# Two probability maps, combined on ScalarE and GpSimd instead of VectorE

## What is computed

```python
s = einsum('bqhmd,bkhmd->bhmqk', qi, k) * ATTN_SCALE        # m: the two maps
s = where(k_pos[None, :] <= q_pos[:, None], s, NEG)         # causal
p = softmax(s, axis=-1)
attn = p[..., 0, :, :] - lam * p[..., 1, :, :]
o = einsum('bhqk,bkhe->bqhe', attn, v)
```

## Time and profile before

| | |
|---|---|
| median of 3 runs | 4023.01 us (4020.77 to 4033.34) |
| profiled execution | 4022.81 us, span 4021.0 us |
| mean granted TensorE clock | 0.911 |
| busy in the span | TensorE 3431.7 us (85%), VectorE 1906.7 (47%), GpSimd 1565.9 (39%), ScalarE 1345.6 (33%) |
| attention loop | from 2616 to about 3060 us of the span |
| VectorE busy in the slices of the page stretch (40 slices of 100.5 us) | 0.8 to 0.9, elsewhere mostly 0.2 to 0.5 |

### The profile page before, as it was taken

The page is one execution under the profiler, slowest core; times in us unless marked ns, Lnnn a source line. Parts: engine busy times, 40 slices in busy tenths (PEclk is TensorE's granted clock), DMA queues, the critical chain, the costliest instruction groups (busy, mean ns, idle before and its releaser), DMA issues. The chain is left out here.

```text
span 4021.0 us, 78382 instructions
## 1 busy us (share of the span) xinstructions
PE 3431.7 (85%) x34057; PEld 3122.6 (78%) x34057; DVE 1906.7 (47%) x2166; ACT 1345.6 (33%) x2067; POOL 1565.9 (39%) x648
## 2 busy tenths in 40 slices
PE   5999695898988268999999999866886889999896
PEld 2899444888888268999999999844555889999896
DVE  3222705455542559337254443089843953512622
ACT  1111122343332124333333343344554433333332
POOL 0111000000000044665656666465402556556563
PEclk8999957899999589999999999978897999999998
DMA  5222024343332163444445466567845344444442
GB/s 193 84 84 79 17 106 145 104 133 120 120 118 77 60 199 102 132 141 139 138 127 150 141 192 184 167 205 252 312 147 163 110 121 137 122 144 141 124 140 69
DMA packets 710476, 546.84 MB, mean 136 GB/s; under 512 B 34762, under 2 KB 667490, under 8 KB 709884
## 3 DMA queue, kind: packets, MB, share of 16 engines
q1 hardware_dynamic: 664182, 473.18, 38.3%
q10 hardware_dynamic: 45606, 67.55, 4.8%
q0 software_dynamic: 352, 1.18, 0.1%
HBM read 471.55 MB, written 70.29 MB: 135 GB/s over the span
## 5 line engine op out<-in xcount | busy, mean ns | idle before, releaser
L1630 POOL TENSOR_TENSOR dense_w_lo<-dense_w_raw,dense_w_hi 128x1024 fp32r<-128x1024 f32 x504 | 1273.5, 2533 | 972.8 <-ACT dense_w_hi L1701 970.6
L1686 PE MATMUL acc<-dense_x_hi,dense_w_hi 128*128 128x344 f32 x2496 | 813.7, 330 | 85.9 <-DVE dense_x_lo L1791 41.6
L1687 PE MATMUL acc<-dense_x_lo,dense_w_hi 128*128 128x344 f32 x2496 | 803.0, 326 | 0.0
L1701 ACT ACTIVATE dense_w_hi<-dense_w_raw 128x1024 fp32r<-128x1024 f32 x504 | 531.2, 1056 | 627.0 <-PE acc L1691 533.8
L1686 PEld LDWEIGHTS acc<-dense_x_hi,dense_w_hi 128*128 128x128 f32 x2496 | 482.9, 193 | 98.2 <-issue 79.6
L1687 PEld LDWEIGHTS acc<-dense_x_lo,dense_w_hi 128*128 128x128 f32 x2496 | 483.0, 193 | 2.5 <-issue 0.9
L1686 PE MATMUL acc<-dense_hid_hi,dense_w_hi 128*128 128x344 f32 x1536 | 483.3, 319 | 0.5 <-DVE dense_hid_lo L1811 0.5
L1687 PE MATMUL acc<-dense_hid_lo,dense_w_hi 128*128 128x344 f32 x1536 | 483.4, 319 | 0.0
L1691 PE MATMUL acc<-dense_x_hi,dense_w_lo 128*128 128x344 f32 x2496 | 448.7, 322 | 1.7 <-POOL dense_w_lo L1630 1.7
L1691 PEld LDWEIGHTS acc<-dense_x_hi,dense_w_lo 128*128 128x128 f32 x2496 | 408.9, 190 | 2.6 <-POOL dense_w_lo L1630 2.6
L750 POOL TENSOR_TENSOR x0T<-nT,levels 128x512 f32<-128x512 f32 x16 | 29.7, 1855 | 748.2 <-DVE bR L1249 748.2
(11 more groups left out here) (385 smaller groups left out, 5922.5 us busy)
## 6 DMA issues: line engine op xcount, KB each, us to landing
dense_w_raw<-in_ffn_w SPq DMA_DIRECT2D x384, 512.0 KB, 4.1
ada_quarter<-in_ada_w SPq DMA_DIRECT2D x40, 1024.0 KB, 10.6
att_k_page<-in_cache_k SPq DMA_DIRECT2D x64, 512.0 KB, 4.2
att_v_page<-in_cache_v SPq DMA_DIRECT2D x64, 512.0 KB, 5.5
scratch_mix<-proj_stage ACTq DMA_DIRECT2D x48, 516.0 KB, 2.7
scratch_mix<-dense_stage ACTq DMA_DIRECT2D x72, 172.0 KB, 2.1
w_raw<-in_a_w_rkv SPq DMA_DIRECT2D x24, 512.0 KB, 4.1
dense_w_raw<-in_a_w_o SPq DMA_DIRECT2D x24, 512.0 KB, 4.4
```

The lines of the kernel that those rows point to most:

```text
L1630: nc.gpsimd.tensor_tensor(wlo[:, i % NW], raw[:, i % NRAW], whi[:, i % NW].bitcast(F32), ALU.subtract).then_inc(S("lo"), 1)
L1686: T_.matmul(out, whi[:, s % NW, k, :], a, start=j.first and k == 0, stop=False)
L1687: T_.matmul(out, whi[:, s % NW, k, :], b, start=False, stop=False)
L1701: A(whi[:, i % NW], raw[:, i % NRAW], ACT.Copy).then_inc(S("hi"), 1)
```

## The change

For unit u - 1 the ratio stays on VectorE. The multiplication of the second map with it moves to ScalarE, in place in `pm`, at the end of the turn behind the output copy. The addition of the first map moves to GpSimd, behind the first page product of turn u (or alone where a turn has none). The addition takes over the wait for the transposes of the map four units earlier. The semaphore `attn` is now counted by GpSimd, and `scaled` is new.

```diff
         @block.gpsimd
         def _(pool):
+            def combine(u):
+                n = blocks(u) * P
+                need(pool, "scaled", u + 1)
+                if u >= 4:
+                    need(pool, "t_mm", nth[attn_rounds(u - 4)[-1]] + 1)
+                nc.gpsimd.tensor_tensor(attn_of(u)[:, 0:n], pm[kind(u)][:, 1, 0:n], pm[kind(u)][:, 0, 0:n], ALU.add).then_inc(S("attn"), 1)
+
             for u in range(END):
+                if not pages_of(u) and 1 <= u <= NU:
+                    combine(u - 1)
                 for j in pages_of(u):
                     b = j // NP
                     pool.wait_ge(S(f"k_in{j % NK}"), 16 * (j // NK + 1))
@@ -2080,6 +2089,8 @@
                         pool.wait_ge(S(f"qb{b % 2}"), 16 * (b // 2 + 1))
                     need(pool, "red", j - NR + 1)
                     nc.gpsimd.tensor_tensor(prod[:, j % NR, :], kp[:, j % NK, :], qb[:, b % 2, :], ALU.mult).then_inc(S("prod"), 1)
+                    if j == pages_of(u)[0] and 1 <= u <= NU:
+                        combine(u - 1)
@@ -2269,17 +2280,12 @@
             def combine(u):
-                kd, c, n = kind(u), u % 4, blocks(u) * P
+                c = u % 4
                 need(dve, "exp", 2 * u + 2)
                 need(dve, "take", u - 3)
                 V.reciprocal(rl[:, c, :], l[:, c, :]).then_inc(S("rl"), 1)
                 need(dve, "rl", u + 1)
                 V.tensor_scalar(w1[:, c, 0:1], rl[:, c, 1:2], l[:, c, 0:1], lam[:, 0:1], ALU.mult, ALU.mult).then_inc(S("ratio"), 1)
-                need(dve, "ratio", u + 1)
-                if u >= 4:
-                    need(dve, "t_mm", nth[attn_rounds(u - 4)[-1]] + 1)
-                V.scalar_tensor_tensor(attn_of(u)[:, 0:n], pm[kd][:, 1, 0:n], w1[:, c, 0:1], pm[kd][:, 0, 0:n], ALU.mult,
-                                       ALU.add).then_inc(S("attn"), 1)
@@ -2450,6 +2456,10 @@
                 if 0 <= w < NU:
                     take(w)
+                if 1 <= u <= NU:
+                    kd, c, n = kind(u - 1), (u - 1) % 4, blocks(u - 1) * P
+                    need(act, "ratio", u)
+                    A(pm[kd][:, 1, 0:n], pm[kd][:, 1, 0:n], ACT.Copy, scale=w1[:, c, 0:1]).then_inc(S("scaled"), 1)
                 h, r = divmod(u, KC)
```

## The result

The changed kernel takes 4122.32 us (median of 4 runs, 4120.45 to 4124.63), the kernel before 4023.37 beside it: ratio 1.0235, 95% interval [1.0219, 1.0251], so 99 us slower by the medians (95 us by the ratio, 88 to 101). The forecast was 4096 us with a range of 4057 to 4132. The side, the mechanism and the range held; the loss was 99 us where I had 73. The range held by its margin alone: the sum's own upper bound was 4121, and the 10 us laid on top of it were meant for the price of the addition, which is not where the miss came from.

A forecast was written before the change was run, and what follows sets the result against it. VectorE was taken to bound the page stretch, and after the change a closed loop over four queues: 332 + 19 = 351 us against 284.9. So 4022.8 + 66 + 7 (units without pages) = 4096 us, range 4057 to 4132.

The forecast's parts named there:

- the sum's own upper bound: Whole kernel: 1.5 us of the TensorE term and the full tail, 4022.8 + 83 + 15 = 4121 us.
- The bound and the gain on offer: Page stretch: VectorE, busy 264 of 285 us, sets the pace; the change would leave it about 158 us.
- The closed loop: Units with pages: addition, page product, page sum, ratio and copy wait in a ring over four queues; 16.2 us per two units.
- TensorE at the low clock: First half of each two-unit round: slow transposes and products exceed the 4.8 us by 1.2; 0.7 taken (0 to 1.5).
- What comes on top per head: Page stretch: squares 5 us, normalisation 6 and column products 8 add 19 us to the 332.
- the squares: Square of the outputs on GpSimd, 1.894 us: about 1.05 us sticks out, five times, 5 us.
- The normalisation: On VectorE per head: 1.225 us and a reciprocal, about 1.4 us, four times, 6 us.
- column products: Eight tiny products of a sample in an odd unit: 1.9 us a sample, four times, 8 us.
- The units without pages: The other 22 units: late ends of three heads 5 us, plus 2 for the rest; +7 us (0 to 15).
- A: Rival, page units: VectorE's relief counts as GpSimd's idle time swallows the waits; 6.1 us a unit, 3995 us; chance 0.07.
- B: Rival, page units: the loop is about as long as VectorE's present work; within 12 us of 4023; chance 0.04.
- C: Rival, page units: TensorE stays at the low level, ScalarE's chain sets both halves; 4133 us and up; chance 0.09.

The follow-up runs named there:

- experiment 2: Changed kernel with GpSimd's addition behind the turn's last page product instead of the first: 4053.79 us; with the addition one turn later: 4017.35 us.
- experiment 6: Changed kernel with VectorE doing maxima and ratio before page sums, an odd turn's second sum moved to the next turn: 4044.95 us, ratio 1.0050.
- experiment 7: Square root at each head's end replaced by a scaled copy: changed kernel 4118.13 us, kernel before 4021.64 us.
- experiment 5: Changed kernel, late addition and ratio first: 4019.13 us; also VectorE combining from unit 42: 4014.89. Kernel before, change in units 42 to 63 alone: 4040.57.

## Why the prediction was right, and where it was off

**The bound and the gain on offer.** Right: VectorE was full and was relieved (264 to 181 us busy), and it brought nothing. I had the busy time at 158 us: the scaling of the maxima kept its 585 ns, because 19 of 41 still met an instruction of GpSimd, which is 17 of the 23 us.

**The closed loop.** Right in kind, by experiments 2 and 6, and in size. By the additions' stamps the steps of head 0 are 10.04, 9.62, 9.20 and 9.83 us from long to short, mean 9.67, where the sum had 9.7; and 6.60, 6.44, 5.88 and 6.48 from short to long, mean 6.35, where it had 5.8 and the 0.7 for TensorE at the low clock. By the start of the long copy against the end of its ratio TensorE's way adds 1.1, 0.8, 0 and 0 us, mean 0.5 and not 0.7, and the way over GpSimd and VectorE is 5.9. Taken over 41 units (five times 64.1 us and one step of 10.04) they make 330.5 us against my 332. Both copies and the long addition cost within 5% of what I took for them (0.98 and 0.55 for 0.95 and 0.53, 1.96 for 1.90). The short addition did not: 0.86 for 0.73, 18% more, because I left out the fixed part that I had named (0.9 with it). So the 332 came out right partly by luck, one term too high and another too low.

**What comes on top per head.** This is the term that was too small: 19 us in my sum, 369.3 - 330.5 = 39 us measured. Item by item, by the step it lengthens against head 0: the squares +1.17 us (I had 1.05), in four heads and not five. The normalisation +2.12 (1.4): it takes 1.99 us instead of 1.225, as the row of L2315 shows. In the changed kernel it starts 0.9 us before the end of a page product that is already running. In the kernel before it started together with a product, kept its 1.22 us, and the product took 3.43 us instead of 2.35. So its price of the earlier trace rows was that of another neighbourhood. The step before it, with sum, root and table loads, +2.1, +1.9, +3.4 and +4.0 in the four heads (nothing in my sum, "covered"). In the first two heads the trace shows the way: the root and its two loads push the next two transposed copies back, 1.6 and 2.8 us later than in the quiet step, and TensorE and the long copy follow them; without the root the step is only 0.6 and 0.7 us over head 0's. In the last two a sample's column products (1.95 and 2.09 us) stand in the same step, ahead of the output copy, and fit the further 1.3 and 2.0 us. That leaves 8 us for the root. Two more samples have their column products in other steps (+1.5 and +1.4), so these come to 6 us, where I had 8. The kernel before pays as much in the steps with the root, 3.4, 2.1, 3.4 and 3.4 us over its head 0, and its 284.9 us hold that; experiment 7 agrees. So the root is no cost of the change, but it was missing from a sum that was built up from quiet rows and then compared with the 284.9.

The remaining 11 us had no term in my sum at all. Some 6 of them stand in the three steps from unit 20 to 23, where the samples' first scores are worked. Another 4.1 is the step from unit 30 to 31, in which GpSimd waits 5.3 us for the query row of experiment 5.

**The units without pages.** 7 us in the sum; 10 to 13 by the stamps and 11 by experiment 5. The value lies in the range of that term (0 to 15), though the interval reaches to 17.

The rest of the 26 us is a start later by 2 us. So: 20 of them from the extras, some 5 from the units without pages, 2 from the start, and 1 or 2 the other way from the loop itself. The step that failed is the one with the extras per head, 39 us for 19: I had taken their prices one by one from rows with other neighbours, called the root with its loads covered although the kernel before already showed that step 3.4 us longer than in the first head, and had neither a transfer nor the samples' scores in the sum.

**The rivals.** A (relief counts) fell. The kernel nearest to it is the one with the addition one turn later, in experiment 2, and even there the gain is 0.27% and not 0.7%: the units with pages take 6.5 us and not 6.1. In that trace ScalarE still waits for ratios, GpSimd for copies and, once, for the query row; how the rest divides among them was not tried. B and C fell. For C: the clock did drop to 0.74, but the first half of the quiet loop came out at 6.35 us, some 0.5 over the way over GpSimd. That these 0.5 us come from TensorE's low clock is argued, from transposes at 0.30 us each after 6 us of idling, and was not tried apart.

## What to carry to other kernels

When work moves to an idle engine, follow its input back through every queue, and see whether it comes round to an instruction behind it in the same queue; if it does, add up the round, for busy shares won't show it. The cure is a turn of slack and not a faster operation: the same instructions one turn later took some 100 us less. And when you cut such a round, look for the second tie before you promise the gain: one of two cut gave 17 us, both gave 75. Before building a new time from quiet rows, lay the first head beside a later one in the trace of before: what the later one has on top must be in the sum as well.

## What the runs showed of the hardware

The normalisation on VectorE (two inputs from SBUF, 1024 columns) took 1.225 us on average in the kernel before and 1.988 us in the four heads with pages of the changed one. There it always starts 3.7 us into two page products on GpSimd that follow each other without a gap (4.65 us for both), and ends 1.1 us after them. In the kernel before it started at the same time as a product, and it was the product that took longer, 3.43 us instead of 2.35. The additions on GpSimd cost 2.34 us for 1024 columns in fp32 and 0.46 us for 128, which is a fixed part of about 0.2 us and 2.1 ns a column. Two loads of ScalarE's tables, 1.28 us each, stand around each square root. A query row of 512 KB, issued behind eight value pages, took 10.2 to 11.2 us to land in the traces of the changed kernel and of three variants, against 5.1 us for the one before it in the changed kernel.
